# Attention columns gated in place, and three tiles of state-space outputs moved on the chip by SyncE

## The reference, cut to what matters

```python
def second_block(x, p, mix_norm, w_in, ..., w_out, ple_norm, w_ple_gate, w_ple_proj):
    ...
        z = rms_norm(h, mix_norm[i]) @ w_in[i]
        q, k, v, gate_a, u, gate_s = jnp.split(z, splits, axis=-1)
        attn = dilated_mixture_attention(q, k, v, q_norm[i], k_norm[i]) * jax.nn.silu(gate_a)
        ssm = s5_glu(u, ..., w_glu[i], b_glu[i]) * jax.nn.silu(gate_s)
        h = h + jnp.concatenate([attn, ssm], axis=-1) @ w_out[i]
        gate = jax.nn.sigmoid(rms_norm(h, ple_norm[i]) @ w_ple_gate[i])
        h = h + gate * (p[i] @ w_ple_proj[i])
```

## Time and profile before

| | |
|---|---|
| median of three runs | 2432.94 us (2432.51 to 2433.62) |
| profiled execution, its own time | 2436.38 us |
| its span in the profile | 2434.6 us |
| PE busy | 2404.3 us, 99% of the span |
| VectorE, ScalarE, POOL busy | 61%, 32%, 12% |
| mean granted clock of PE | 0.999 |

### The profile page before, as it was taken

One profiled execution on the slowest core, in us unless ns is written; L12 is line 12 of the kernel. 1 busy time (PEld: TensorE's weight loads), 2 busy tenths in 40 slices (PEclk: granted clock), 3 DMA queues, 4 the chain that ended last, 5 costly groups with the idle time before them and its releaser, 6 DMA issues.

```text
span 2434.6 us, 40237 instructions
## 1 busy us (share of the span) xinstructions
PE 2404.3 (99%) x15655; PEld 1813.4 (74%) x15655; DVE 1494.1 (61%) x3590; ACT 780.5 (32%) x1836; POOL 303.9 (12%) x491
## 2 busy tenths in 40 slices
PE   9999999999999999999999999999999999999999
PEld 4577688777788686577788776868678865766767
DVE  3268776699876664444453477757778665545454
ACT  3247411277721123333300066113212272221211
POOL 2001000000051000000051023320000003141000
PEclk9999999999999999999999999999999999999999
DMA  8130001122033121211001112532341126253411
GB/s 304 44 109 24 19 35 35 36 79 83 14 104 113 61 96 69 72 51 42 17 23 41 35 52 46 102 110 87 122 154 35 44 84 174 83 191 115 165 69 52
DMA packets 80365, 194.21 MB, mean 80 GB/s; under 512 B 8364, under 2 KB 19312, under 8 KB 79136
## 3 DMA queue, kind: packets, MB, share of 16 engines
q0 software_dynamic: 28864, 99.57, 13.1%
q1 hardware_dynamic: 50560, 91.69, 10.9%
q10 hardware_dynamic: 752, 0.38, 0.1%
HBM read 148.05 MB, written 42.07 MB: 78 GB/s over the span
## 4 chain that ended last, share of the span: by engine, by line
PE 92%; DVE 2%; DMA 2%; issue 1%; POOL 1%; ACT 1%; DVEq 0%; SPq 0%; POOLq 0%; ACTq 0%
PE psum L1749 39%; PE psum L1799 11%; PE psum L2123 8%; PE psum L2280 6%; PE psum L2216 4%; PE psum L2277 4%; PE psum L1927 3%; PE psum L2044 2%; PE psum L2362 2%; PE psum L1735 1%; PE psum L1716 1%; PE psum L2456 1%; PE psum L2474 1%; PE psum L1875 1%; DMA RQ<-in_ev_w_ada 1%
## 5 line engine op out<-in xcount | busy, mean ns | idle before, releaser
L3994 ACT ACTIVATE RP<-RP,small 128x1280 f32<-128x1280 f32 (+12 forms) x286 | 247.7, 868 | 167.1 <-DVE small L3456 166.4
L1799 PE MATMUL psum<-RQ 64*128 64x256 f32 (+5 forms) x1200 | 256.6, 482 | 0.9 <-DVE RX L3536 0.5
L3456 DVE CUSTOM_DVE_ANT_0 RP<-psum,small 128x256 f32<-128x256 f32 (+1 forms) x362 | 192.5, 571 | 52.8 <-PE psum L1799 48.8
L2123 PE MATMUL psum<-RW,hT 128*128 128x512 f32 (+3 forms) x608 | 218.1, 512 | 0.0
L1799 PEld LDWEIGHTS psum<-RQ 64*128 64x128 f32 (+1 forms) x1200 | 132.7, 188 | 75.0 <-issue 51.9
L2123 PEld LDWEIGHTS psum<-RW,hT 128*128 128x128 f32 x608 | 128.1, 216 | 72.7 <-issue 54.6
L1749 PE MATMUL psum<-RW,hT 128*128 128x256 f32 x736 | 167.2, 379 | 0.0
L1749 PEld LDWEIGHTS psum<-RW,hT 128*128 128x128 f32 x736 | 139.4, 190 | 22.5 <-issue 2.2
L1749 PE MATMUL psum<-RW,RP 128*128 128x256 f32 x576 | 136.1, 379 | 0.0
L2280 PE MATMUL psum<-RQ,RP 128*128 128x128 f32 x1024 | 125.5, 278 | 0.8 <-DVE RP L3478 0.8
L2280 PEld LDWEIGHTS psum<-RQ,RP 128*128 128x128 f32 x1024 | 119.2, 192 | 4.1 <-DVE YR L3512 0.9
(11 more groups left out here) (618 smaller groups left out, 4349.5 us busy)
## 6 DMA issues: line engine op xcount, KB each, us to landing
RW<-in_w_in SPq DMA_DIRECT2D x7, 2048.0 KB, 8.0
RW<-in_od_w_ada SPq DMA_DIRECT2D x6, 2048.0 KB, 8.2
RW<-in_ev_w_in SPq DMA_DIRECT2D x5, 2048.0 KB, 7.9
RW<-in_od_w_in SPq DMA_DIRECT2D x5, 2048.0 KB, 7.9
RQ<-in_ev_w_ada SPq DMA_DIRECT2D x8, 1024.0 KB, 14.7
RX<-in_x POOLq DMA_DIRECT2D x12, 512.0 KB, 6.9
RW<-in_ev_w_ada SPq DMA_DIRECT2D x2, 2048.0 KB, 8.7
RW<-in_ev_w_out SPq DMA_DIRECT2D x2, 2048.0 KB, 9.1
```

The costliest lines, as they stand in the source:

```text
L1799: last = pe.matmul(ring.bank(f)[:, 0:pc["w"]], q, kk[:, keys], start=i == 0, stop=i == len(u["qk"]) - 1)
L2123: last = pe.matmul(main.bank(f)[:, c0:c0 + nc_], lhs_of(st["lhs"], j["t"], kk), w, start=kk == 0, stop=kk == kn - 1)
L3456: drained(ring, dve.tensor_tensor_reduce(pair_slot(st, u, lane)[:, pc["at"]:pc["at"] + pc["w"]], ring.bank(f)[:, 0:pc["w"]], add, -scale, ...
L3994: fn(pr, pr, ACT.Exp, bias=mins[:, at, lane, n - 1:n], scale=-1.0, accum_out=total).then_inc(s_pexp, 1)
```

## The change

1. The gates 8 to 11 are multiplied straight into `gated_columns`, as 12 to 15 were. `gated_dil` and its transfers go. To make room, `glT` moves to `RP[:, 0:4096]`, and the sums of the second group of token columns take the place of the first group's, so they are made behind `quads[1]` and not inside it.
2. SP moves y of the tiles 0 to 2 from `y_loc` to the tile buffers in 24 transfers of 16 rows of 2 KB, when `s_yglu` comes. POOL stores only the other tiles' y to `y_ssm`. It waits for its own store and for all 24 before it loads `p`.
3. POOL loads the gate tiles 0 to 2 before it waits for `s_yglu`, the x tiles 0 and 1 right behind the store of y, tile 3 of y and gate behind gate 13, and `w_proj` behind the tile loads of the next stage.

```diff
-        token_columns = [new_columns(hT3[:, :, 512 * g:512 * g + 512], [RP[:, c:c + 1024] for c in at])
-                         for g, at in enumerate(((4096, 5120, 6144), (0, 1024, 2048)))]
+        token_columns = [new_columns(hT3[:, :, 512 * g:512 * g + 512], [RP[:, c:c + 1024] for c in (4096, 5120, 6144)])
+                         for g in range(2)]
...
-        glT = RQ[:, 4096:8192].rearrange("p (k t) -> p k t", k=4)
+        glT = RP[:, 0:4096].rearrange("p (k t) -> p k t", k=4)
...
             for n in range(n_weights):
                 w = weights[n]
+                if n == out_mix["w"][1]:
+                    sp.wait_ge(s_yglu, 1)
+                    for i in range(3):
+                        for r in range(8):
+                            sp.dma_start(y_tile(i)[r:P:8, :], y_loc[16 * i:16 * i + 16, r, :]).then_inc(s_first_y[i], 16)
...
                 gp.wait_ge(s_gstore[n % 3], 16 * (n // 3 + 1))
-                gp.dma_start(y_tile(i), y_ssm[rows, :]).then_inc(s_yg[i % 3], 16)
+                if i >= 3:
+                    gp.dma_start(y_tile(i), y_ssm[rows, :]).then_inc(s_yg[i % 3], 16)
                 gp.dma_start(gate_tile(i), gate_2[rows, :]).then_inc(s_yg[i % 3], 16)
...
-                    for i in range(4):
+                    for i in range(2 if st["gated_here"] else 0, 4):
                         load_x(ts[i], src_of(ts[i]))
                     for i, j in enumerate(ts):
                         if st["gated_here"] and i == 0:
-                            for n in range(3, 7):
+                            for n in range(4, 7):
                                 load_y_and_gate(ts[n])
+                            gp.dma_start(w_proj, kview(io["w_ple_proj_2"][0])).then_inc(s_pw, 16)
...
-                        if a < 4:
-                            attention_step(gp.tensor_tensor(slot, slot, y, ALU.mult))
-                            gp.dma_start(gated_dil[:, e["b"], :], slot).then_inc(s_gstore[n % 3], 16)
-                        else:
-                            gp.tensor_tensor(gated_columns[:, e["b"], e["tok"]], slot, y, ALU.mult).then_inc(s_late, 1)
-                            gp.wait_ge(s_late, a - 3)
+                        gp.tensor_tensor(gated_columns[:, e["b"], e["tok"]], slot, y, ALU.mult).then_inc(s_late, 1)
+                        gp.wait_ge(s_late, a + 1)
...
-                    gp.wait_ge(s_yglu, 1)
-                    gp.dma_start(y_ssm.rearrange("(m s) c -> m s c", s=8), y_loc).then_inc(s_yssm, 16)
-                    for n in (9, 10, 11):
-                        gp.wait_ge(s_gstore[n % 3], 16 * (n // 3 + 1))
-                    gp.dma_start(gated_columns[:, :, 0:512], gated_dil).then_inc(s_columns, 16)
-                    gp.wait_ge(s_yssm, 16)
                     for j in out_mix["tiles"][0:3]:
                         load_y_and_gate(j)
+                    gp.wait_ge(s_yglu, 1)
+                    gp.dma_start(y_ssm.rearrange("(m s) c -> m s c", s=8)[48:P], y_loc[48:P]).then_inc(s_yssm, 16)
+                    for j in out_mix["tiles"][0:2]:
+                        load_x(j, x_out[j["t"] * P:(j["t"] + 1) * P, :])
+                    gp.wait_ge(s_yssm, 16)
+                    for i in range(3):
+                        gp.wait_ge(s_first_y[i], 16 * 8)
                     gp.dma_start(p_nat, io["p_2"][0, 0].rearrange("(t p) c -> p t c", p=P)).then_inc(s_p, 16)
-                    store_gate(st["gates"][12])
-                    gp.dma_start(w_proj, kview(io["w_ple_proj_2"][0])).then_inc(s_pw, 16)
-                    for e in st["gates"][13:]:
+                    for e in st["gates"][12:14]:
+                        store_gate(e)
+                    load_y_and_gate(out_mix["tiles"][3])
+                    for e in st["gates"][14:]:
                         store_gate(e)
...
             gate_quad(st["quads"][0], second_rows)
-
-            def second_columns(spot):
-                if spot == 0:
-                    for i in range(4):
-                        combined_weights(st["columns"][1], i)
-
-            gate_quad(st["quads"][1], second_columns)
+            gate_quad(st["quads"][1], lambda spot: None)
+            for i in range(4):
+                combined_weights(st["columns"][1], i)
...
-                    dve.wait_ge(s_yg[i], 32)
+                    dve.wait_ge(s_yg[i], 16)
+                    dve.wait_ge(s_first_y[i], 16 * 8)
                     sig(tt(y_tile(i), y_tile(i), gate_tile(i), M), s_prod)
...
                         def free(e):
                             n = e["n"]
-                            if n == 15:
-                                dve.wait_ge(s_late, 1)
+                            if n >= 11:
+                                dve.wait_ge(s_late, n - 10)
                             else:
                                 dve.wait_ge(s_gstore[n % 3], 16 * (n // 3))
```

More of the change, by code:

```diff
@@ L140, in build @@
         inverse_dil = dram("inverse_dil", [8, S])
-        gated_dil = dram("gated_dil", [P, 4, 512])
         gate_2 = dram("gate_2", [S, 512])
@@ L252, in build @@
         s_att_step = sem("attention_columns_step")
-        s_columns = sem("gated_columns_loaded")
         s_late = sem("gated_columns_ready")
@@ L260, in build @@
         s_prod = sem("gated_y_ready")
+        s_first_y = [sem(f"first_y{i}_moved") for i in range(3)]
         s_out = sem("out_stored")
@@ L2003, in _ @@
                     if st["gated_here"]:
-                        pe.wait_ge(s_columns, 16)
+                        pe.wait_ge(s_late, 4)
                     for pair in st.get("pairs_out", []):
@@ L2019, in _ @@
                                     if pair["at"] == 2:
-                                        pe.wait_ge(s_late, 4)
+                                        pe.wait_ge(s_late, 8)
                                 seven_products(pair["quads"][c], turn_some)
@@ L3006, in rows_combined @@
                     if plain:
-                        dve.wait_ge(s_columns, 16)
+                        dve.wait_ge(s_late, 4)
                         for j in pair["tiles"]:
@@ L3025, in out_pairs @@
                         for i in range(3):
-                            dve.wait_ge(s_gstore[i], 16 * len(range(i, 12, 3)))
-                        dve.wait_ge(s_late, 4)
+                            dve.wait_ge(s_gstore[i], 16 * len(range(i, 8, 3)))
+                        dve.wait_ge(s_late, 8)
                     for c in range(2):
@@ L3180, in product @@
                         i = j["at"]
-                        dve.wait_ge(s_yg[i % 3], 32 * (i // 3 + 1))
+                        dve.wait_ge(s_yg[i % 3], 16 + 32 * (i // 3))
+                        if i < 3:
+                            dve.wait_ge(s_first_y[i], 16 * 8)
                         sig(tt(y_tile(i), y_tile(i), gate_tile(i), ALU.mult), s_prod)
@@ L3840, in _ @@
                         for i in range(3):
-                            act.wait_ge(s_gstore[i], 16 * len(range(i, 12, 3)))
-                        act.wait_ge(s_late, 4)
+                            act.wait_ge(s_gstore[i], 16 * len(range(i, 8, 3)))
+                        act.wait_ge(s_late, 8)
                     def out_rows(pair):
```

## The result

The changed kernel takes 2440.31 us (median of 8 runs, 2439.18 to 2441.35) against 2433.81 us of the kernel before (8 runs beside it, 2432.51 to 2434.58). The ratio is 1.0029, 95% interval 1.002 to 1.0038: **slower by 6.5 us, 0.29%**. The forecast was 2435.2 us in a range of 2427 to 2441.5, with "no change" at 0.65 and "slower" at 0.21. The time lies in the range, near its upper end, but above the 2430 to 2438 us given for the likeliest case; and 6.5 us is more than the 4.9 us called "no change", so it is the less likely side that came. The profiled execution took 2440.48 us for a span of 2438.7, 4.1 us more than the span of before.

What follows compares the result with a forecast made beforehand. TensorE, busy 99%, was taken to bound the kernel, so only its idle or low-clock stretches matter. Removing 7.71 us and adding 9.95 (7.1 stall, 2.85 clock) gave +2.2 us: 2435.2 from a 2432.94 median, range 2427 to 2441.5.

Steps and rivals of the forecast that it cites:

- no change: Outcome within about 0.2%, 4.9 us, of the kernel before, from a step of 0.53 to 0.83 us; chance 0.65.
- slower: Outcome of a time more than about 0.2%, 4.9 us, above the kernel before; chance 0.21 over all slower rivals.
- likeliest case: SP's issue step between 0.53 and 0.83 us, no distinguishable change in time, 2430 to 2438 us; chance 0.65.
- The chain: Before quad 3: POOL, VectorE and PE have no slack, so PE waits for whatever POOL is late.
- What I put at nothing: In-place gates, later column sums beside GLU, earlier x loads and w_out_2's load: no gain or cost on PE's path.
- The old stall goes: In w_out_2's first stage, PE's 4.9 us wait for tile 3's gated product disappears, with the low clock behind it.
- 7.71 us removed: Gain from tile 3 loaded behind gate 13: 4.9 us wait plus 2.85 us low clock in w_out_2.
- The step between issues: SP's 24 transfers of y: 0.718 us from issue to issue, taken from L1357's burst.
- The new stall: PE turns tile 0 at 2184.6 instead of 2177.45, after SP's 24 pieces: 7.1 us.
- throttled: Rival: POOL's transfers slow SP's issues; average step 1.0 us gives net +8.7 us (2441.6); chance 0.17.
- The low clock behind the new stall: PE's work after its wait at tile 0 runs at low clock, costing 2.85 us, as behind the earlier wait.
- Its strongest reading, one piece after the other: Rival: SP's pieces don't overlap, each paying 2.1 us; 31.8 us above the forecast (2467); chance 0.01.

Runs made afterwards that it cites:

- run with two issuers: Changed kernel with 12 of SP's 24 pieces issued by ScalarE's queue instead: 2436.79 us, ratio 1.0008 to the kernel before.
- quiet order: Changed kernel, x tiles 0 and 1 in the next stage, POOL's store of y behind the wait for SP's pieces: 2436.7 us with 24 pieces, 2427.71 with three.
- three quiet transfers: Changed kernel with x tiles in the next stage, POOL's store of y after SP's moves, and three 256 KB transfers replacing 24: 2427.71 us, ratio 0.9972.
- two tiles: Changed kernel with SP moving y of two tiles only (16 pieces), tile 2 going through DRAM: 2435.84 us, ratio 1.0009.
- late x tiles: Changed kernel with x tiles 0 and 1 loaded in the next stage, not beside SP's burst: 2440.73 us, ratio 1.0027.
- three transfers: Changed kernel with three transfers of SP, one for each tile, in place of 24, POOL's order unchanged: 2433.34 us, ratio 0.9998.

## Why the prediction was right, and where it was mis-sized

**The chain: right.** POOL, VectorE and PE stand nose to tail; From POOL's issue of p to PE's turn I had 5.09 us, and the profile has 2187.02 - 2181.93 = 5.09. What frees the chain is gate 12's place: with it moved ahead, 12.6 us go and SP's burst is as long as before.

**What I put at nothing: right.** GLU without a gap, no wait for w_out_2, none for the gates in place. The run without the pieces shows it: 2429.07. For w_out_2 the margin was smaller than I said. I priced its load by the 7.8 us of a store; it took 10.7 us to landing in the profile of before, 8.8 in the changed kernel and 14.7 in the run with two issuers, against a cover of 15.8.

**The old stall goes: right in kind, mis-sized.** The term "7.71 us removed" was made from one execution. Moving tile 3 alone gives 5.4 us by the medians, and the second profile of the kernel before has 5.35. The step was taken against its own profiled time, as a sum must be, but that time, 2436.38, lay 3.4 us above the median of the runs shown. I named the difference and then carried it over unchanged, as if it had nothing to do with the stall that I priced; most of it was that stall.

**The step between issues: mis-sized.** I took 0.718 us; it was 0.810, which makes 2.1 us over 23 steps. The new stall was 9.6 us instead of 7.1. Most of what is left is a term that I had put at nothing without a reason: the last piece landed at 2179.33 + 2.0 = 2181.33, and POOL issued p only 0.60 us later. The steady part was better known than I used it: about 0.635 us from start to start, as in the trace of L1357 (eight steps from 1942.46 to 1947.56), though the pieces are half the size. The long issues are the rest. With the rival "throttled" I had the right suspicion and the wrong evidence: I took the two long members of L1357 for what POOL's stores may cost, and charged about the same here. POOL's store of y costs more (2.0, 2.2 and 0.9 us in place of 3 x 0.59), and the long members of L1357 have another companion (see the last section). At 0.81 this is at the edge of that rival, which I let decide from 0.83 on.

**The low clock behind the new stall:** 2.85 us forecast. The turn costs 1.11 - 0.66 = 0.45, the two groups of eight products 1.73 + 0.32, in all 2.5.

The sum with what was measured: 9.6 + 2.5 - 5.4 = +6.7 us, against the measured 6.5; with the first profile's 7.71 it is +4.4, against 4.1 between the profiled spans. So the two terms account for the miss of 4.3 us in the difference: about 2.5 from the longer stall and 2.3 from the cheaper removal, less 0.35 of clock. The time itself is missed by 5.1 us (2440.31 against 2435.2), since the kernel before has a median of 2433.81 beside it and I started from 2432.94.

**The range: in part luck.** All of these errors but the clock point the same way. What kept the time inside was the room at the upper end, left for a step of up to about 1.0 us; the step came out lower, and the cheaper removal filled that room, which no rival had priced.

**Two rules against the traces.** The Trainium skill (DMA: Bandwidth & Descriptors, "Queues, rings and completion order") lets each DMA engine change between its queues packet by packet. By that rule POOL's store hardly slows SP's pieces, and the step stays at 0.635. The traces agree neither on the step nor on the landing: with the store beside it the burst of 24 is 19.1 to 19.6 us long, without it 16.3, and the second piece lands 7.3 us after its start in the changed kernel and 2.0 in the quiet order. Whether the packets take turns all the same, and the delay arises elsewhere, isn't shown.

The Trainium skill (same page, "Measured (HBM→SBUF, 128 partitions, SWDGE, issued from GpSimd)") wants batches of 1 MiB or more and calls transfers under 64 KB dominated by descriptors. Its rows are of loads from DRAM that GpSimd issues, and these are moves on the chip that SP issues, but the direction agrees: in the quiet order POOL gets on at 2178.59 behind 24 pieces and at 2168.39 behind three with the same bytes. Its strongest reading, one piece after the other, didn't come.

**The version to keep.** The changed kernel with gates 12 and 13 ahead of the wait (2427.68), or with three quiet transfers (2427.71), beats the kernel before by 0.26 to 0.28%, and the changed kernel by 0.5%. The simple move of tile 3 in the kernel before (2428.54) gives nearly all of it. The moves on the chip bring about 1 us beyond that, and the intervals overlap.

## What to carry to other kernels

When a transfer is split into many, cost the issuing engine's step times the count, and then ask which instruction of which queue waits for the last one, and what stands behind it. Here 24 cheap issues made PE wait 9.6 us only because one engine waited for all of them ahead of work that didn't need them. And before a stall read from one profile is priced, compare that execution's own time with the median: if it is 3 us above, the stall may be one of the things that vary.

## What the runs showed of the hardware

- **Issue time doesn't follow size.** Pieces of 32 KB took 0.59 us each, as those of 64 KB; of three of 256 KB the first two took 0.60 to 0.68, the third 1.80 and 1.90 in the two runs.
- **A large store of one queue delays another queue's issue.** With POOL's store of y just begun (1.25 MB, 1.5 with two tiles), the 3rd to 5th issues took 2.0 to 2.2, 2.1 to 2.2 and 0.9 to 1.6 us in each of the four kernels with a burst of 16 or 24 beside it, and on ScalarE's queue at the same moments. Without it they took 0.59. The pair that shows it is the late x tiles against the quiet 24: POOL has the store alone beside the burst in one, nothing in the other. But the third of three quiet transfers took 1.90 us as well, with its own two of 256 KB ahead of it. By what the issue is held isn't shown.
- **One long issue in each long burst comes with an instruction transfer.** It is the 18th in the changed kernel (1.43 us at 2174.69) and the 23rd in the quiet one (1.79 us at 2174.17), with nothing of POOL's under way there. The three other kernels with a burst of 16 or 24 have one there too (1.11 to 1.62 us, between 2174.38 and 2175.89). The DMA view of each such stretch has one packet on q8, a queue of instructions, and the rest of the two bursts has none. The two long members of L1357 (at 1948.20 and 1958.51) have such a packet too. The packet also comes where SP issues nothing, between 2176 and 2179 in the kernel before and between 2173 and 2176 with three transfers, so the pieces don't bring it. No run moved it or took it away: this is a coincidence seen seven times, and not a cause shown. The row, from the quiet kernel, 2173 to 2176:

```profile
q8 instruction: 1, 0.02, 3.2%
```

- **Idle times of nearly one length came with and without a low clock.** 3.73 us of waiting in the second profile of before were followed by a granted clock of 0.50, and 3.50 us with three transfers by none (1.00 in all slices, the turn in 0.66 us). The second is an exception within its own kernel: it comes from the one execution of eleven with a mean granted clock of 1.000, 1.8 us below the median.

```profile
2180.50 0.66 PE L1774 MATMUL psum<-ident,RQ 128*128 128x128 f32 x4 [3.50 <-DVE RQ L2680]
```
